# Retention blocks: the state wait behind the intra product, and three rows of the residual stream returned inside the last head

## The chip, the core and the metric

The kernel runs on one core of one Trainium2 chip. The metric is the device time of one execution in microseconds (us), the median over runs. The engines are TensorE (PE: matrix products; PEld: its weight loads), VectorE (DVE), ScalarE (ACT), GpSimd (POOL) and SyncE (SP, which here only issues transfers). Each runs its own instructions in order and they meet through semaphores. SP and ACT each feed one queue of transfers; the same 16 DMA engines serve both. The matrix products run in a format of reduced precision on operands split into a high and a low part, so that one product of full precision is three: high by high, high by low and low by high.

## The reference, cut to what matters

A decoder trunk of four layers works on 1024 prompt positions and 8 sample positions (T = 1032 columns) of width 1024. Layers 0 and 3 are multi-scale retention, layer 1 is differential attention, layer 2 a gated linear recurrence. Each layer is x + W_out(mixer(RMSNorm(x)) * silu(gate)). The change touches layers 0 and 3. There the prompt is cut into eight blocks of 128 positions, and for each of four heads (keys of 256, values of 512) a state S is carried from block to block:

```
s = einsum('bihd,bjhd->bhij', q, k) * decay
o = einsum('bhij,bjhv->bihv', s, v)                 # intra product
o = o + einsum('bihd,bhdv->bihv', q, S0) * q_dec    # state product
S = exp(C*lg) * S0 + einsum('bjhd,bjhv->bhdv', k * k_dec, v)
...
out = (rms_norm(o) * silu(g)) @ w_out
x = x + out
```

The 8 sample positions have one state each, read and written in device memory.

## The kernel before, in words

**Units and chunks.** Activations lie transposed: width on partitions, positions along the free dimension, cut into three chunks of 384, 384 and 264 columns. A unit is 128 output columns of a weight matrix; TensorE makes one unit chunk by chunk, each chunk 8 tiles of three products (`unit_chunk`, lines 301 to 303). Weights go through two raw slots: SP loads one (`load_w`, line 240), ACT copies its high part (`split_hi`, line 248), POOL subtracts for the low part (`split_lo`, line 257), and then the raw slot is free for the next load. Results of a unit go through two PSUM banks in turn.

**A head of retention.** `ret_pe`, `ret_act` and `ret_dve` run the same loop of 36 steps per head (12 units of 3 chunks: 2 of keys, 4 of values, 2 of queries, 4 of the gate). In a step TensorE makes one chunk, and from step 24 on it does in the gate units' shadow, for t = step - 24:
- the four transposes of the output of block t-2 (line 944),
- for block r = t-1: three intra products into the bank OB (953 to 955), for r > 0 the state product on top of it (959, two halves of the key width), then the new contribution to the state into SB0 and SB1 (964 to 966),
- the scores of block t (line 985).

ACT takes block r on: it squares and sums OB (1064), and with DVE's reciprocal root (lines 600 to 607) it scales OB into `onb` (1074), which frees OB. DVE masks the scores (1137), scales the queries (`qdT`, 1144), subtracts for the low part of the scores (`sdl`, 1148), and then folds SB0 and SB1 into the state `St` (1159 and 1160). Semaphores: `r_sd` tells that `sdl` is done, `r_on` that OB is free, `r_qd` that `qdT` is done, `r_su` that `St` holds the block before (and SB0 and SB1 are free), `r_st` that line 966 is done. Before line 953 TensorE waits for `r_sd`, `r_on` and `r_su`; before line 959 for `r_qd`. In step 26 ACT issues four loads of sample states (line 1048) before it goes on with the block. ACT also stores the gate (1028), the normalised output (1058), the sample states (1080) and, after the last block, the prompt's state (1094).

**Where the residual stream goes.** The residual stream `xT` has 8 rows of 128 partitions by 1032 columns. During a retention layer its first six rows (`AWAY_ROWS`) are lent out: `vtl` and `ktl`, the low parts of values and keys, lie there, block after block. The rows come back at the beginning of the output projection (`x_reload`, line 759), from the input in layer 0 and from a copy in device memory (`x_save`) in layer 3. Each row has a semaphore `x_back`, and DVE waits for it before the first addition to that row (`residual_dve`, line 445).

**The output projection.** `out_sp`, `out_act`, `out_dve` and `out_pe` run it in two halves of the input width. Its input, normalised output times gate, is staged from device memory chunk by chunk (`stage_load`, line 414; two slots), DVE multiplies it (`stage_dve`, line 435), ACT copies the high part (334), DVE subtracts for the low part (341). `out_order` begins with units 0 and 1 chunk by chunk, then the other units one after the other. On DVE the order is fixed: fill chunk 0, half of chunk 1, then additions (line 445) with the remaining half fills between them. Each addition frees a PSUM bank.

**What SP issues.** At the end of the last head `out_sp` issues in this order: the first W_out load (it waits for the raw slot); after `r_st` of the last block (`ret_stage_wait`) the stage loads of chunk 0, then row 0; the second W_out load; after the prompt's state has landed (line 707) the stage loads of chunk 1, then row 1; row 2 and the third W_out load; row 3; the stage loads of chunk 2 and the fourth W_out load; row 4, the next half's stage loads, a W_out load; row 5, a W_out load; and so on.

Of the kernel before, what the change touches and what calls it, by code (L numbers as in the profile page):

```python
# [145 lines left out]
def trunk(nc, A, LAYERS=4):  # L146
    ctx = ExitStack()
    with ctx:
# [3 lines left out]
        def sem(name):  # L152
            return ctx.enter_context(nc.semaphore(name))
# [56 lines left out]
        dve_own = sem("dve_own")  # L210
        stage_ld = sems("stage_ld", 4)
        tab_ld, page_cp = sem("tab_ld"), sem("page_cp")
        x_saved, x_back = sem("x_saved"), sems("x_back", KT)

        CR = 2
        CR_PS = 3
# [221 lines left out]
        def residual_dve(dve, unit, q, j, c, final, sqb, sqn, back):  # L438

            c0, w = CHUNKS[c]  # L440
            dve.wait_ge(unit_ps, out_ps(unit, q))
            dve.wait_ge(unit_ev, out_ev(unit, q) - 1)
            if back is not None and c == 0 and j < AWAY_ROWS:
                dve.wait_ge(x_back[j], back)
            nc.vector.tensor_tensor(xT[:, j, c0:c0 + w], bank[q % 2][:, 0:w], xT[:, j, c0:c0 + w], ALU.add)\  # L445
              .then_inc(unit_ev, 1)
            if final:
                dve.wait_ge(sq_done, sqn + 1)
                nc.vector.tensor_tensor(ss[:, c0:c0 + w], ss[:, c0:c0 + w], sqb[:, q % 2, 0:w], ALU.add)\
                  .then_inc(ss_done, 1)  # L450
# [177 lines left out]
        def ret_sp(sp, lay):  # L628
            j_, U, R = lay // 3, UNIT_AT[lay], RAW_AT[lay]
            win, wout = A["ret_w_in"][j_], A["ret_w_out"][j_]  # L630

            def weights(h, js):
                for j in js:
                    col = (h * RDK + (RQK + j * P) if j < 2 else h * RDV + (2 * RQK + (j - 2) * P) if j < 6 else
                           h * RDK + (j - 6) * P if j < 8 else h * RDV + (2 * RQK + RV + (j - 8) * P))
                    load_w(sp, Pos(R, h, RU_IN), j, w_block(win, 0, KT, col))

            def value_rows(h, bs):

                n8, ntr = Pos(8 * RH * j_, h, 8), Pos(RTR * RH * j_, h, RTR)  # L640
                if 0 in bs:
                    sp.wait_ge(r_te, done(ntr.at(17)))
                    sp.wait_ge(r_sn, prior(n8.at(0)))
                    sp.dma_start(v_d, vs[0:NS, :]).then_inc(r_vst, 16)
                    sp.wait_ge(r_vst, Pos(RH * j_, h, 1).at(0) * 16 + 16)
                for b in bs:
                    if b >= 4:
                        sp.wait_ge(r_sn, done(n8.at(b - 4)))
                    sp.dma_start(vbr[:, b % 4, :], v_d[b:b + 1, :].to_broadcast([P, RDV])).then_inc(r_vld[b % 4], 16)

            def page_copies(ns):

                for n in ns:
                    ids = sp.value_load(ptab[0:1, n:n + 1])
                    b, g = divmod(n, PAGES)
                    for cache, dst in ((A["cache_kt"], kc_d), (A["cache_vt"], vc_d)):
                        reg = nc.s_assert_within(ids, 0, cache.shape[1] - 1,
                                                 skip_runtime_bounds_check_because="page ids are rows of the cache")
                        sp.dma_start(dst[b:b + 1, :, :, g, :].rearrange("a h p c -> (a h p) c"),
                                     cache[0, bass.ds(reg, 1), :, :, :].rearrange("a h p c -> (a h p) c"))\  # L660
                          .then_inc(page_cp, 16)

            def head(h):
                sp.wait_ge(r_fo, h + (RH * j_ + 1))
                sp.dma_start(hc, A["c_ret"][bass.ds(h, 1), :, :].rearrange("a p n -> (a p) n")).then_inc(r_hc, 16)
                for j in range(2, 10):
                    weights(h, (j,))
                    if lay == 0:
                        page_copies(range(16 * h + 2 * (j - 2), 16 * h + 2 * (j - 1)))
                    if j == 8:  # L670
                        value_rows(h, range(0, 4))
                weights(h, (10,))
                value_rows(h, range(4, NS))
                weights(h, (11,))

            if lay == 0:
                sp.wait_ge(tab_ld, 16)
            weights(0, (0, 1) if lay else (1,))
            if lay:
                for k in range(KT - 4, AWAY_ROWS):  # L680
                    x_save(sp, UNIT_AT[lay] - KT, k)
                sp.wait_ge(h_raw, fill_tiles(FILL_AT[lay] - 1, 2) + FILL_K[FILL_AT[lay] - 1])
                sp.wait_ge(ss_done, KT * NC_ * (lay + 1))
            sp.dma_start(rsel, A["c_sel"][:, P + 8:P + 16]).then_inc(r_sel, 16)
            for h in range(RH - 1):
                head(h)
                weights(h + 1, (0, 1))
            head(RH - 1)
            out_sp(sp, lay, wout, U + 48, R + 48, [(FILL_AT[lay] + 1, 0), (FILL_AT[lay] + 2, KT)], ret_stage_wait,
                   late_wait=ret_end_wait)  # L690

# [30 lines left out]
        def out_sp(sp, lay, wout, U, R, fills, stage_wait, loaded=0, after=None, late_wait=None):  # L722

            st = stage_of(lay)
            for x, (f, k0) in enumerate(fills):
                kt = FILL_K[f]
                raw = Pos(R + 8 * x)
                if x == 0:
                    for j in range(2):
                        if j >= loaded:  # L730
                            load_w(sp, raw, j, w_block(wout, k0 * P, kt, j * P), kt)
                        if stage_wait is not None:
                            stage_wait(sp, lay, j)
                            stage_load(sp, st, f, k0, j)
                        if lay in (0, 3):
                            x_reload(sp, lay, j)
                    if after is not None:
                        after(sp)
                for j in range(2 if x == 0 else 0, KT):
                    if lay in (0, 3) and x == 0 and j < AWAY_ROWS:  # L740
                        x_reload(sp, lay, j)
                    if lay == 2 and LAYERS > 3 and x + 1 == len(fills) and j >= 4:
                        x_save(sp, U + 8 * x, j - 4)
                    if j == 3:
                        sp.wait_ge(h_raw, fill_tiles(f, 0) + FILL_K[f])
                        stage_load(sp, st, f, k0, 2)
                    if j == 4 and x + 1 < len(fills):
                        sp.wait_ge(h_raw, fill_tiles(f, 1) + FILL_K[f])
                        if late_wait is not None:
                            late_wait(sp, lay)  # L750
                        stage_load(sp, st, *fills[x + 1], 0)
                        sp.wait_ge(h_raw, fill_tiles(f, 2) + FILL_K[f])
                        stage_load(sp, st, *fills[x + 1], 1)
                    load_w(sp, raw, j, w_block(wout, k0 * P, kt, j * P), kt)

        def x_reload(sp, lay, k):

            src = A["x_cols"][k * P:(k + 1) * P, :] if lay == 0 else x_d[k:k + 1, :, :].rearrange("a p t -> (a p) t")
            sp.dma_start(xT[:, k, :], src).then_inc(x_back[k], 16)

        def x_save(sp, U, k):

# [102 lines left out]
        def out_dve(dve, ch, lay, U, fills, last_layer, scale, beside=None, begun=False):  # L865
# [4 lines left out]
            for x, (f, k0) in enumerate(fills):  # L870
# [8 lines left out]
                            clear_sums(dve, ch, lay)  # L879
                    stage_dve(dve, st, f, 1, scale, 0)  # L880
                for q, (j, c) in enumerate(out_order(more or final)):
                    residual_dve(dve, unit, q, j, c, final, sqb, sqn, 16 * (lay // 3 + 1) if lay in (0, 3) and x == 0 else None)
                    sqn += final
                    if q in FILL_BEHIND:
                        stage_dve(dve, st, f, FILL_BEHIND[q][0], scale, FILL_BEHIND[q][1])
# [33 lines left out]
        def ret_pe(pe, lay):  # L919
            f = FILL_AT[lay]  # L920
            def head(h, first):
                unit, raw, n1, n8, ntr = ret_places(lay, h)
                for s in range(36):
# [22 lines left out]
                    if 0 <= t - 1 < NBLK:  # L946
# [2 lines left out]
                            pe.wait_ge(r_te, done(ntr.at(17)))  # L949
                        pe.wait_ge(r_sd, done(n8.at(r)))  # L950
                        pe.wait_ge(r_on, prior(n8.at(r)))
                        pe.wait_ge(r_su, prior(n8.at(r)))
                        nc.tensor.matmul(OB[:, :], sdh[:, r % 2, :], vth[:, r, :], start=True, stop=False)
                        nc.tensor.matmul(OB[:, :], sdh[:, r % 2, :], vtl[:, r, :], start=False, stop=False)
                        last = nc.tensor.matmul(OB[:, :], sdl[:, r % 2, :], vth[:, r, :], start=False, stop=(r == 0))
                        if r:
                            pe.wait_ge(r_qd, done(n8.at(r)))
                            for x in range(2):
                                last = nc.tensor.matmul(OB[:, :], qdT[:, r % 2, x, :], St[:, x, :], start=False,  # L959
                                                        stop=(x == 1))  # L960
# [1278 lines left out]
```

## Time and profile before

| | |
|---|---|
| median of 3 runs | 3273.43 us (3272.81 to 3280.8) |
| profiled execution | 3276.99 us, span 3275.2 us, mean granted clock 0.986 |
| PE, PEld busy | 3120.3 us (95%), 2838.0 us (87%) |
| DVE, ACT, POOL busy | 1372.2 us (42%), 1267.7 us (39%), 561.9 us (17%) |
| transfers | 459.78 MB, mean 140 GB/s |

The span runs from the first to the last instruction of the profiled execution. A busy share is the time in which an engine had an instruction, over the whole span; stages differ. Matmuls are pipelined and their ends are modelled: a matmul's shown time overlaps that of the next. Layer 0 ends near 990 us and layer 3 begins near 2330 us; the last heads' blocks run from about 711 to 778 us and from 2999 to 3066 us.

### The profile page before, as it was taken

What the parts mean: (1) busy time and instruction counts of PE and PEld (TensorE: products, weight loads), DVE (VectorE), ACT (ScalarE), POOL (GpSimd) and SP (SyncE); (2) the same over time, 40 slices, a digit from 0 to 9 for tenths busy, and PEclk for the clock granted to TensorE, in tenths of its full rate; (3) what the DMA queues carried; (4) which work ended last, traced back from release to release, by engine and by line L of the source; (5) the groups of instructions that cost most, each with busy time, mean ns of one, the idle gap of its engine ahead of it and who ended that gap; (6) DMA issues with size and microseconds to landing.
All of it is one profiled execution on the core that took longest, in us unless ns stands there. A gap on an engine that the chain in (4) does not pass through costs nothing.

```text
span 3275.2 us, 51546 instructions
## 1 busy us (share of the span) xinstructions
PE 3120.3 (95%) x19978; PEld 2838.0 (87%) x19978; DVE 1372.2 (42%) x3480; ACT 1267.7 (39%) x2709; POOL 561.9 (17%) x432
## 2 busy tenths in 40 slices
PE   6999999998998999999979899989799999999899
PEld 4989898997997888888859899979798989899799
DVE  3241514226344444444445777763524151422631
ACT  4332423334234555455543455532433332333321
POOL 1112021111211111011101223222111211111121
PEclk8999999999999999999999999999999999999999
DMA  5848586776413444444453122232234242425742
GB/s 164 256 151 248 168 245 194 213 240 224 145 56 116 139 136 155 142 147 143 141 187 100 34 64 63 64 106 82 63 125 129 88 148 89 151 78 163 240 138 80
DMA packets 531892, 459.78 MB, mean 140 GB/s; under 512 B 25091, under 2 KB 464387, under 8 KB 531651
## 3 DMA queue, kind: packets, MB, share of 16 engines
q1 hardware_dynamic: 425570, 334.75, 32.8%
q10 hardware_dynamic: 106080, 121.74, 10.8%
q8 instruction: 160, 2.62, 0.3%
q14 instruction: 82, 0.66, 0.1%
HBM read 354.39 MB, written 169.14 MB: 160 GB/s over the span
## 4 chain that ended last, share of the span: by engine, by line
PE 79%; DVE 10%; issue 4%; ACT 4%; DMA 2%; ACTq 1%; SPq 1%; POOL 0%; DVEq 0%
PE psum L301 20%; PE psum L302 20%; PE psum L303 20%; PE psum L959 3%; PE psum L1419 2%; DVE Hl L341 2%; PE psum L1392 2%; DVE hraw L385 2%; PE psum L936 1%; DVE hraw L435 1%; PE psum L1408 1%; PE psum L1931 1%; PE psum L1462 1%; PE psum L976 1%; PE psum L1431 1%
## 5 line engine op out<-in xcount | busy, mean ns | idle before, releaser
L301 PE MATMUL psum<-Hh,Wh 128*128 128x384 f32 (+1 forms) x4896 | 1633.6, 334 | 92.9 <-DVE Hl L341 31.6
L302 PE MATMUL psum<-Hl,Wh 128*128 128x384 f32 (+1 forms) x4896 | 1574.7, 322 | 0.0
L303 PE MATMUL psum<-Hh,Wl 128*128 128x384 f32 (+1 forms) x4896 | 1574.0, 321 | 0.0
L301 PEld LDWEIGHTS psum<-Hh,Wh 128*128 128x128 f32 x4896 | 931.5, 190 | 147.7 <-issue 55.0
L257 POOL TENSOR_TENSOR Wl<-wraw,Wh 128x512 fp32r<-128x512 f32 (+1 forms) x416 | 533.3, 1303 | 2518.3 <-ACT Wh L248 2517.2
L302 PEld LDWEIGHTS psum<-Hl,Wh 128*128 128x128 f32 x4896 | 932.3, 190 | 6.2 <-issue 0.3
L303 PEld LDWEIGHTS psum<-Hh,Wl 128*128 128x128 f32 x4896 | 930.2, 190 | 0.0
L248 ACT ACTIVATE Wh<-wraw 128x512 fp32r<-128x512 f32 (+1 forms) x416 | 235.1, 615 | 267.3 <-PE psum L303 148.2
L445 DVE TENSOR_TENSOR xT<-psum,xT 128x384 f32<-128x384 f32 x168 | 86.3, 514 | 294.8 <-PE psum L303 294.1
L334 ACT ACTIVATE Hh<-hraw 128x384 fp32r<-128x384 f32 (+1 forms) x252 | 116.5, 489 | 153.8 <-DVE hraw L435 82.4
L1020 ACT ACTIVATE hraw<-psum 128x384 f32<-128x384 f32 (+1 forms) x96 | 44.0, 458 | 279.3 <-PE psum L303 279.3
L1166 DVE SCALAR_TENSOR_TENSOR arena<-arena 128x512 f32<-128x512 f32 x128 | 98.4, 820 | 106.5 <-ACT arena L1069 106.5
L1128 DVE TENSOR_TENSOR vtl<-psum,vth 128x384 fp32r<-128x384 f32 (+1 forms) x96 | 48.6, 506 | 212.0 <-ACT vth L1042 212.0
L1660 ACT ACTIVATE arena<-arena 128x256 f32<-128x256 f32 (+7 forms) x128 | 98.2, 769 | 86.7 <-DVE arena L1725 86.7
L341 DVE TENSOR_TENSOR Hl<-hraw,Hh 128x384 fp32r<-128x384 f32 (+1 forms) x252 | 119.5, 510 | 13.7 <-ACT Hh L334 13.2
L1122 DVE SCALAR_TENSOR_TENSOR ktl<-psum,arena,kth 128x384 fp32r<-128x384 f32 (+1 forms) x48 | 27.5, 573 | 216.8 <-ACT kth L1039 216.8
L1721 DVE CUSTOM_DVE_ANT_0 arena<-psum,arena 128x256 f32<-128x256 f32 (+7 forms) x128 | 91.9, 754 | 47.0 <-PE psum L1392 45.5
L1026 ACT ACTIVATE arena<-psum 128x384 f32<-128x384 f32 (+1 forms) x96 | 44.0, 458 | 166.7 <-PE psum L303 166.7
L959 PE MATMUL psum<-arena 128*128 128x512 f32 x224 | 105.2, 592 | 0.0
L600 DVE TENSOR_SCALAR arena<-arena 128x1 f32<-128x1 f32 x72 | 11.1, 154 | 208.7 <-ACT hraw L1064 208.7
L1074 ACT ACTIVATE arena<-psum,arena 128x512 f32<-128x512 f32 x64 | 44.1, 689 | 117.0 <-DVE arena L607 117.0
L456 ACT ACTIVATE arena<-xT 128x384 f32<-128x384 f32 (+1 forms) x72 | 35.4, 491 | 132.2 <-DVE xT L445 132.2
(212 smaller groups left out, 3164.7 us busy)
## 6 DMA issues: line engine op xcount, KB each, us to landing
wraw<-in_ret_w_in SPq DMA_DIRECT2D x96, 512.0 KB, 4.4
scratch_kc<-in_cache_kt SPq DMA_DIRECT2D x64, 512.0 KB, 6.4
scratch_vc<-in_cache_vt SPq DMA_DIRECT2D x64, 512.0 KB, 6.7
arena<-in_state_ret ACTq DMA_DIRECT2D x64, 512.0 KB, 6.9
out_ret_state_sample<-arena ACTq DMA_DIRECT2D x64, 512.0 KB, 5.1
arena<-scratch_kc SPq DMA_DIRECT2D x64, 512.0 KB, 4.3
arena<-scratch_vc SPq DMA_DIRECT2D x64, 512.0 KB, 4.5
scratch_on<-arena ACTq DMA_DIRECT2D x78, 256.0 KB, 2.4
```

Of the source, the lines that this page charges most:

```text
L248: act.activation(Wh[:, j % 2, x], wraw[:, j % 2, x], ACT.Copy).then_inc(w_hi, 1)
L257: pool.tensor_tensor(Wl[:, j % 2, x], wraw[:, j % 2, x], Wh[:, j % 2, x].bitcast(F32), ALU.subtract)\
L301: nc.tensor.matmul(out, hi, xh, start=(k == 0), stop=False)
L302: nc.tensor.matmul(out, hi, xl, start=False, stop=False)
L303: last = nc.tensor.matmul(out, lo, xh, start=False, stop=(k == kt - 1))
L334: act.activation(Hh[:, k, c0:c0 + w], hraw[:, n % HR, 0:w], ACT.Copy).then_inc(h_hi, 1)
L341: nc.vector.tensor_tensor(Hl[:, k, c0:c0 + w], hraw[:, n % HR, 0:w], Hh[:, k, c0:c0 + w].bitcast(F32), ALU.subtract).then_inc(h_lo, 1)
L445: nc.vector.tensor_tensor(xT[:, j, c0:c0 + w], bank[q % 2][:, 0:w], xT[:, j, c0:c0 + w], ALU.add)\
L959: last = nc.tensor.matmul(OB[:, :], qdT[:, r % 2, x, :], St[:, x, :], start=False, stop=(x == 1))
L1166: last = nc.vector.scalar_tensor_tensor(sring[:, b % 4, x, :], vbr[:, b % 4, :], kT[:, x, SEQ + b:SEQ + b + 1], sring[:, b % 4, x, :], ALU ...
L1660: act.activation(x, x, ACT.Exp, bias=nm2[:, s % 2, m:m + 1], accum_out=(l8[:, s:s + 1], l1[:, s % 2:s % 2 + 1])[m]).then_inc(d_ex, 1)
L1721: nc.vector.tensor_tensor_reduce(out=(S0[t % 3], S1[t % 2])[m][:, 0:W], in0=SSC[m][:, 0:W], in1=strip[:, SEQ - W:SEQ], scale=1.0, scalar=- ...
```

## The change

TensorE's wait for `r_su` moves from line 953 to behind line 955, so that the three intra products come before it. For blocks r > 0 it then stands with the wait for `r_qd` before line 959; for r = 0 it stands before line 964. Rows 0, 1 and 2 are returned by SP at the end of the last head's own issues, behind `r_st` of blocks 2, 4 and 6, when `vtl` and `ktl` of the blocks that lie in a row have been read; the first W_out load comes behind them. Rows 3, 4 and 5 are issued ahead of the third, fourth and fifth W_out load, one place earlier each. Two rows share one `x_back` semaphore, and an addition waits for both.

```diff
-        x_saved, x_back = sem("x_saved"), sems("x_back", KT)
+        x_saved, x_back = sem("x_saved"), sems("x_back", 3)
...
             if back is not None and c == 0 and j < AWAY_ROWS:
-                dve.wait_ge(x_back[j], back)
+                dve.wait_ge(x_back[j // 2], back)
...
             head(RH - 1)
+            for k in range(3):
+                sp.wait_ge(r_st, done(8 * RH * (j_ + 1) - 8 + 2 * k + 2))
+                x_reload(sp, lay, k)
             out_sp(sp, lay, wout, U + 48, R + 48, [(FILL_AT[lay] + 1, 0), (FILL_AT[lay] + 2, KT)], ret_stage_wait,
                    late_wait=ret_end_wait)
...
                             stage_load(sp, st, f, k0, j)
-                        if lay in (0, 3):
-                            x_reload(sp, lay, j)
                     if after is not None:
                         after(sp)
                 for j in range(2 if x == 0 else 0, KT):
-                    if lay in (0, 3) and x == 0 and j < AWAY_ROWS:
-                        x_reload(sp, lay, j)
+                    if lay in (0, 3) and x == 0 and j + 1 < AWAY_ROWS:
+                        x_reload(sp, lay, j + 1)
...
-            sp.dma_start(xT[:, k, :], src).then_inc(x_back[k], 16)
+            sp.dma_start(xT[:, k, :], src).then_inc(x_back[k // 2], 16)
...
-                    residual_dve(dve, unit, q, j, c, final, sqb, sqn, 16 * (lay // 3 + 1) if lay in (0, 3) and x == 0 else None)
+                    residual_dve(dve, unit, q, j, c, final, sqb, sqn, 32 * (lay // 3 + 1) if lay in (0, 3) and x == 0 else None)
...
                         pe.wait_ge(r_sd, done(n8.at(r)))
                         pe.wait_ge(r_on, prior(n8.at(r)))
-                        pe.wait_ge(r_su, prior(n8.at(r)))
                         nc.tensor.matmul(OB[:, :], sdh[:, r % 2, :], vth[:, r, :], start=True, stop=False)
                         nc.tensor.matmul(OB[:, :], sdh[:, r % 2, :], vtl[:, r, :], start=False, stop=False)
                         last = nc.tensor.matmul(OB[:, :], sdl[:, r % 2, :], vth[:, r, :], start=False, stop=(r == 0))
+                        pe.wait_ge(r_su, prior(n8.at(r)))
                         if r:
                             pe.wait_ge(r_qd, done(n8.at(r)))
```

## Rows read from the trace of the kernel before

**Rows 1.** The profile's chain that ended last, shares of the span by engine
```profile
PE 79%; DVE 10%; issue 4%; ACT 4%; DMA 2%; ACTq 1%; SPq 1%; POOL 0%; DVEq 0%
```
**Rows 2.** Waits of TensorE, whole span: total us, times, longest us
```profile
PE psum L953 <- DVE arena L1160: 13.2, 24, 0.7
```
**Rows 3.** TensorE's timeline, block 6 of layer 0's last head: start, us
```profile
763.69 0.60 PE L944 MATMUL psum<-ident,arena 128*128 128x128 f32 x4
...
764.59 0.39 PE L955 MATMUL psum<-vth,sdl 128*128 128x512 f32 x1
764.82 1.88 PE L959 MATMUL psum<-arena 128*128 128x512 f32 x4
...
767.69 0.39 PE L966 MATMUL psum<-vth,ktl 128*128 128x512 f32 x1
```
**Rows 4.** The same, block 7, behind a chunk of 264 columns
```profile
771.28 0.60 PE L944 MATMUL psum<-ident,arena 128*128 128x128 f32 x4
772.44 0.47 PE L953 MATMUL psum<-vth,sdh 128*128 128x512 f32 x1 [0.56 <-DVE arena L1160]
...
773.21 1.88 PE L959 MATMUL psum<-arena 128*128 128x512 f32 x4
```
**Rows 5.** The same, block 2, behind a chunk of 384 columns
```profile
727.94 0.60 PE L944 MATMUL psum<-ident,arena 128*128 128x128 f32 x4
...
729.76 1.88 PE L959 MATMUL psum<-arena 128*128 128x512 f32 x4
```
**Rows 6.** Stretches: five engines' busy us (instructions), granted clock, DMA share, GB/s
```profile
772.00:774.00 2.00, 1.56 (x5) 1.05 (x6) 1.62 (x3) 0.60 (x1) 0.00 (x0) 1.00 0.36 127
3106.00:3110.00 4.00, 3.89 (x20) 3.89 (x21) 3.36 (x10) 1.53 (x4) 0.00 (x0) 0.62 1.04 375
```
**Rows 7.** DVE's timeline, first fill of chunk 2, layer 0
```profile
814.51 1.12 DVE L435 SCALAR_TENSOR_TENSOR hraw<-arena 128x264 f32<-128x264 f32 x3 [3.94 <-DMA arena<-scratch_g]
```
**Rows 8.** TensorE's timeline, unit 0, chunk 2, layers 0 and 3
```profile
818.00 0.39 PE L301 MATMUL psum<-Hh,Wh 128*128 128x264 f32 x1 [2.73 <-DVE xT L445]
...
3106.11 0.39 PE L301 MATMUL psum<-Hh,Wh 128*128 128x264 f32 x1 [2.82 <-DVE xT L445]
```
**Rows 9.** DVE's timeline, blocks 2 and 7 of layer 0's last head
```profile
728.10 0.74 DVE L1160 SCALAR_TENSOR_TENSOR arena<-arena,psum 128x512 f32<-128x512 f32 x1
...
770.69 0.29 DVE L1148 TENSOR_TENSOR sdl<-arena,sdh 128x128 fp32r<-128x128 f32 x1 [0.42 <-ACT sdh L1077]
...
771.55 0.74 DVE L1160 SCALAR_TENSOR_TENSOR arena<-arena,psum 128x512 f32<-128x512 f32 x1
```
**Rows 10.** TensorE's weight loads, block 6 of layer 0's last head
```profile
764.59 0.41 PEld L959 LDWEIGHTS psum<-arena 128*128 128x128 f32 x2
```
**Rows 11.** SP's timeline, last head and output projection, layer 0: start, issue us
```profile
730.39 0.38 SPq L240 DMA_DIRECT2D wraw<-in_ret_w_out  x1
776.52 0.37 SPq L414 DMA_DIRECT2D arena<-scratch_on  x1
...
780.35 1.81 SPq L759 DMA_DIRECT2D xT<-in_x_cols  x1
...
793.82 0.37 SPq L414 DMA_DIRECT2D arena<-scratch_on  x1
...
796.38 1.85 SPq L759 DMA_DIRECT2D xT<-in_x_cols  x2
...
798.76 5.04 SPq L759 DMA_DIRECT2D xT<-in_x_cols  x1
```
**Rows 12.** ACT's timeline, split of the first W_out weight, layer 0
```profile
779.31 1.15 ACT L248 ACTIVATE Wh<-wraw 128x512 fp32r<-128x512 f32 x2
```
**Rows 13.** SP's waits between 700 and 850 us: total us, times, longest
```profile
SPq L707 <- DMA out_ret_state_prompt<-arena: 10.7, 1, 10.7
```
**Rows 14.** Transfers, whole span: issues, KB each, median us to landing
```profile
out_ret_state_prompt<-arena ACTq DMA_DIRECT2D x8, 512.0 KB, 3.2
...
xT<-in_x_cols SPq DMA_DIRECT2D x6, 516.0 KB, 10.8
```

## The prediction, made before the change was run

> **What bounds the kernel now.** I read the chain of waits first: 79% of the span's last-ending chain is TensorE, so time that TensorE stands still is the currency [rows 1]. Next the list of TensorE's waits: block products, line 953, stood still 24 times for the vector engine's state update (line 1160), 13.2 us in all [rows 2]. TensorE's timeline then shows what that costs. A head runs eight retention blocks, one behind each chunk of its last units. In a block that doesn't wait, line 959 starts 1.13 us behind the transposes of line 944 (763.69 to 764.82), with the three intra products (953 to 955) between [rows 3]. Behind a short, 264 column chunk the same way takes 1.93 us (771.28 to 773.21) [rows 4]: 0.80 us is lost where the list shows 0.56, since the transposes' modelled end hides part of it. Going through all 64 blocks of the eight heads, the 24 are always the third, fifth and eighth of a head. The fifth and eighth stand behind short chunks (16 blocks, of which [rows 4] shows one); the third stands behind a long chunk, and ScalarE is late there, since it issues four state loads first (8 blocks; 727.94 to 729.76 is 1.82, so 0.69 lost) [rows 5].
>
> Where the output projection begins I read SyncE's timeline, then the waits of SyncE, DVE and TensorE there. The DMA is busy throughout, at 375 GB/s [rows 6]. The third chunk of the staged inputs comes so late that DVE stands still 3.94 us for it [rows 7], the residual addition is queued behind that fill, and TensorE, which needs the addition's PSUM bank, stands still 2.73 us in layer 0 and 2.82 in layer 3 [rows 8].
>
> **Part 1: the wait for the state, behind the three intra products.** No instruction is added; one wait moves on TensorE's queue, in 64 blocks. The three products read neither state nor state banks; the two of line 959 read the state, and line 964 overwrites the banks. What was late is the update's end at 771.55+0.74 = 772.29 [rows 9], and line 953 started at 772.44, 0.15 later [rows 4]. With the wait moved, the products start behind the transposes and line 959 has two lower limits: its own queue, 771.28+1.13 = 772.41, and the state, seen at 772.44. Its weights are loaded 0.23 ahead of its matmul (764.59 against 764.82) [rows 3, 10]; if that load stands behind the wait and nothing covers it, 772.44+0.23 = 772.67. So it starts between 772.44 and 772.67 instead of 773.21: 0.54 to 0.77 gained. I take 0.66, the middle, times 16 = 10.6. In the third block the limits are 727.94+1.13 = 729.07 and 728.10+0.74+0.15 = 728.99 to 729.22, against 729.76: 0.54 to 0.69, I take 0.62, times 8 = 5.0. Part 1 is 15.6 us.
>
> What is late next? The products also wait for sdl, done at 770.69+0.29 = 770.98, 0.30 before even the transposes start [rows 4, 9]. So the state stays last, by some hundredths, now at line 959. Blocks are not coupled backwards: ScalarE's and DVE's work on a block is released by TensorE's line 959 and 966, so it moves along. Bounds: the two unknowns are how much of the weight load shows and whether the pipe drains. If it drains fully, line 955's last 0.39-0.23 = 0.16 [rows 3] is lost as well: 24 x (0.54-0.16) = 9.1. The far end is 16 x 0.77 + 8 x 0.69 = 17.8. In the other 40 blocks the semaphore is up before and the moved wait costs nothing, as the wait for qdT, already at this place, costs nothing: line 959's weights load right with line 955's matmul, no idle time shown [rows 10].
>
> The Trainium skill (TensorE: Matmul & The Clock Gate, Single matmul latency and Back-to-back issue gap) speaks against: a 512 column product that can't overlap its drain takes (398+512)/2.4 = 379 ns, not 216. As an estimate by that page, if each of the 24 blocks drained, part 1 would be 24 x 0.163 = 3.9 less, 11.7; no row here shows a wait at line 959.
>
> **Part 2: rows 0 to 2 of the residual stream return in the last head.** In layers 0 and 3 SyncE issues them behind blocks 2, 4 and 6 of the last head (about 733, 750 and 768.1: the last is line 966's end, 767.69+0.39, 3.26 behind line 959's start [rows 3]; the first 729.76+3.26 [rows 5]); before, at 780.35 and 796.38 [rows 11]. Three transfers of 516 KB, 1.41 us each at 375 GB/s. Their cover: SyncE issued nothing between 730.39 and 776.52 [rows 11], and the DMA ran at a share of 0.36, 127 GB/s [rows 6]. I cost them at nothing; if contention reached a transfer of that stretch it would be ScalarE's stores, whose buffers it needs again only two blocks, some 17 us, later.
>
> Queued behind the waiting SyncE is one thing: the first W_out load, which moves from 730.39 to 768.1 and behind row 2. ScalarE splits that weight at 779.31 [rows 12]. Two transfers of 0.5 MB are 2.8 us at 375 GB/s; with as much again for other traffic and latency they land near 774, 5 us early: nothing. GpSimd's half of the split follows ScalarE's and moves with nothing. The additions now wait for two rows on one semaphore: rows 0 and 1 are back some 40 us before the first addition, row 3 goes out near 796 and the addition that needs it comes behind 818 [rows 8].
>
> Stream rows 3, 4 and 5 each move up one place, in front of the loads of W_out 2, 3 and 4. So between the second chunk's stage load (793.82) and the third's stand two rows (3, 4) instead of three (1, 2 and 3) [rows 11]: 1.41 us earlier. And row 0 no longer stands among what SyncE issues ahead of the second chunk's load. That load waited 10.7 us for the store of the prompt state to land [rows 13], a store with a median of 3.2 us [rows 14]; it lands when the saturated DMA has drained, so up to 1.41 us earlier again. The third chunk comes 1.4 to 2.8 us earlier, against 2.73 and 2.82 of TensorE's waits: I take 2.4 per layer, nearer the upper end, because the store's landing is what ended that wait [rows 13]. Behind layer 3's wait the granted clock averages 0.62 over 4 us, so most of them at 1.2 GHz instead of 2.4 [rows 6]; that cost up to 0.38 x 4 = 1.5 us, which goes only if the wait does, and I take 0.6. Part 2 is 2 x 2.4 + 0.6 = 5.4, bounds 0 (the third chunk held by something else) and 2.73+2.82+1.5 = 7.1.
>
> The Trainium skill (DMA: Bandwidth & Descriptors, Queues, rings and completion order) says that each DMA engine takes turns between the queues, packet by packet. By that page row 0 in SyncE's queue would hardly delay ScalarE's store, the shift would be 1.4 and part 2, as an estimate, 2 x 1.4 = 2.8. The store's long landing here [rows 13, 14] speaks against even turns.
>
> **Sum.** 15.6+5.4 = 21.0 us. The profiled execution took 3276.99, its span 3275.2 with 1.8 around it, 3.6 above the median of the runs shown. 3276.99-21.0 = 3256.0 in its terms; from the median, 3273.4-21.0 = 3252.4, call it 3252.
>
> **Rivals.**
> A. Only part 1 pays: the DMA stays full, and the third chunk is no earlier. For it: every window there is full. Against: fewer bytes ahead of it. 3273.4-15.6 = 3258. Chance 0.14.
> B. The pipe drains at the new place: part 1 is 9.1, sum 14.5, 3259. For it: 772.44 is a few hundredths behind 772.41, so line 959 does wait. Against: TensorE loads those weights early wherever it isn't blocked [rows 10]. Chance 0.10.
> C. W_out 0 comes late. If it and row 2 each took 10.8 us, the median of the returning rows in the crowded stretch [rows 14], in turn, it would land at 768.1+21.6 = 789.7, 10.4 behind ScalarE's split; ScalarE evicts TensorE's banks in the same queue, so TensorE stands still. Twice 10.4 eats 20.8 of 21.0: 3273, no change. Against: the stretch isn't crowded. Chance 0.04.
> D. Part 1 doesn't do what it says: another wait of line 953 stands as late, and only part 2 is left, 3268. Against: sdl is done before the transposes start [rows 4, 9]. Chance 0.04.
> E. Slower: the wait between lines 955 and 959 breaks the overlap in all 64 blocks, not only where it blocks: 0.16 drain, 0.41/2 = 0.20 weight load [rows 10], 0.15 semaphore, 0.51 x 64 = 33 us, 3273.4-21.0+33 = 3285. It decides from 21.0/64 = 0.33 us per block. Against: the qdT wait at that place. Chance 0.05.
> The forecast has 0.63; its own range is 3247 to 3257.
>
> **How the numbers follow.** Best sum 17.8+7.1 = 24.9, 3248.5; worst of A and B together 9.1, 3264. The range 3245 to 3265 takes these in with 1 to 3 us for the spread of the median, and leaves out C, D and E. A change of 0.3% is 9.8 us, about what can be told from none: forecast, A and B are faster (0.87), C and D the same (0.08), E slower (0.05).
>
> **What would show it.** Line 953's 24 waits are gone, and a wait for line 1160 shows at line 959, if any, of a tenth of a us; short-chunk blocks go from 944 to 959 in 1.15 to 1.4 us. If that stays near 1.9, D; if unblocked blocks grow past 1.13, E. The first W_out load stands near 766, and ScalarE's split isn't preceded by a DMA wait (else C). DVE's wait for the third chunk falls from 3.94 to 1.1 to 2.5 us and TensorE's 2.73 and 2.82 to under 1.4 (else A). The forecast is wrong if part 1 measures under 9 us.

## The result

The changed kernel takes 3254.83 us in the median of 4 runs (3250.32 to 3255.57), beside 3274.26 for the kernel before (4 runs): a ratio of 0.9934, with a 95% interval of 0.9923 to 0.9946, so 19.4 us less. The forecast was 3252, with a range from 3245 to 3265. A second comparison, with 5 runs beside 15 of before, gave 3251.72 against 3275.94, 0.9922 (0.9909 to 0.9936), 24.2 us less.

**The blocks.** The list of TensorE's waits of the changed kernel has no row for line 953 any more, where it had 24 waits [rows 2]. One for the state is left, at the state product (now line 960), twice:

```profile
PE psum L960 <- DVE arena L1161: 0.7, 2, 0.4
```

TensorE's timeline of the changed kernel, block 7 of layer 0's last head, behind a chunk of 264 columns (to be set beside [rows 4]), and below it the last product of the same block in the kernel before:

```profile
760.74 0.60 PE L945 MATMUL psum<-ident,arena 128*128 128x128 f32 x4
...
761.88 1.93 PE L960 MATMUL psum<-arena 128*128 128x512 f32 x4
...
764.81 0.40 PE L967 MATMUL psum<-vth,ktl 128*128 128x512 f32 x1
```
```profile
776.09 0.39 PE L966 MATMUL psum<-vth,ktl 128*128 128x512 f32 x1
```

From transposes to state product it takes 1.14 us, where it took 1.93, and where a block that waits for nothing takes 1.13 [rows 3]. Two more rows of the same block of the changed kernel show why: DVE's state update, and TensorE's weight load.

```profile
761.03 0.74 DVE L1161 SCALAR_TENSOR_TENSOR arena<-arena,psum 128x512 f32<-128x512 f32 x1
```
```profile
761.82 0.30 PEld L960 LDWEIGHTS psum<-arena 128*128 128x128 f32 x2 [0.23 <-DVE arena L1161]
```

The state is done at 761.77, and the weights of the state product load 0.05 later, at 761.82. Unblocked they would load at 761.65, 0.23 ahead of the matmul. So the load is late, as the row's wait says, and the first matmul behind it isn't: it starts at 761.88, 0.01 behind its own queue's limit of 760.74+1.13 = 761.87. Over the 56 blocks with a state product, the way from the transposes to that product sums to 82.2 us before and 65.0 now, 17.2 less.

Not all of that is kept, since the late load shows one matmul later. The four matmuls of the state product take 1.93 us here and 1.88 where nothing waits [rows 3]. The last product of the block starts 764.81-760.74 = 4.07 behind the transposes: before it was 776.09-771.28 = 4.81, and in a block that doesn't wait it is 767.69-763.69 = 4.00 [rows 3]. Up to their last products the 56 blocks gain 16.2 us.

**The output projection.** SyncE's timeline of the changed kernel, layer 0 (start, us of issue; to be set beside [rows 11]):

```profile
723.32 0.33 SPq L760 DMA_DIRECT2D xT<-in_x_cols  x1
...
757.59 0.33 SPq L760 DMA_DIRECT2D xT<-in_x_cols  x1
757.96 0.43 SPq L240 DMA_DIRECT2D wraw<-in_ret_w_out  x1
765.23 0.38 SPq L414 DMA_DIRECT2D arena<-scratch_on  x1
...
781.48 0.36 SPq L414 DMA_DIRECT2D arena<-scratch_on  x1
```

Chunk 1's stage loads go out 16.25 us behind chunk 0's, where it was 17.30 (793.82-776.52). DVE's and TensorE's timelines at the third chunk, layer 0 and then layer 3 (to be set beside [rows 7, 8]):

```profile
801.20 1.12 DVE L435 SCALAR_TENSOR_TENSOR hraw<-arena 128x264 f32<-128x264 f32 x3 [1.91 <-DMA arena<-scratch_g]
```
```profile
804.68 0.39 PE L301 MATMUL psum<-Hh,Wh 128*128 128x264 f32 x1 [0.70 <-DVE xT L445]
...
3085.79 0.39 PE L301 MATMUL psum<-Hh,Wh 128*128 128x264 f32 x1 [0.36 <-DVE xT L445]
```

From the last state product to this point it takes 42.80 us in layer 0 (before: 818.00-773.21 = 44.79) and 42.48 in layer 3 (before 45.16). The granted clock behind it in layer 3 (engines' busy us, then clock, DMA share, GB/s; to be set beside [rows 6]) stays at 2.4 GHz, 1.00 instead of a mean of 0.62:

```profile
3085.80:3089.80 4.00, 3.88 (x29) 3.67 (x30) 3.66 (x10) 1.90 (x5) 0.00 (x0) 1.00 1.06 375
```

ScalarE's split of the first W_out weight follows its neighbour without a wait, so the load that moved from 730.39 to 757.96 is in time:

```profile
767.94 0.20 ACT L1088 ACTIVATION_READ_ACCUMULATOR arena<-psum 128x1 f32 x1
768.03 1.15 ACT L248 ACTIVATE Wh<-wraw 128x512 fp32r<-128x512 f32 x2
```

**The account of the two traces.** The span is 3253.8 against 3275.2, 21.4 less: 16.0 in the retention heads (layer 0 from 607.74 to 598.85, layer 3 from 607.67 to 600.55, each from the first transposes of an output to the last state product), 2.0 and 2.7 where the projections begin, 1.1 from layer 3's third chunk to the end, 2.4 ahead of these; against that it took 2.8 more between layer 0's third chunk and layer 3's heads.

### The profile page after: what moved, and what is told of

Its sections match the earlier page's. It is cut to its first block, busy times and chain, and to the rows that moved or that the text cites. A ratio compares the mean times of both kernels' runs of the same rounds, so it can differ in the third digit from the quotient of the medians.

```text
span 3253.8 us, 51594 instructions
## 1 busy us (share of the span) xinstructions
PE 3120.5 (96%) x19978; PEld 2838.7 (87%) x19978; DVE 1369.5 (42%) x3480; ACT 1267.6 (39%) x2709; POOL 560.8 (17%) x432
## 4 chain that ended last, share of the span: by engine, by line
PE 84%; DVE 8%; ACT 3%; issue 3%; DMA 2%; SPq 1%; POOL 0%; ACTq 0%; DVEq 0%
PE psum L301 21%; PE psum L302 21%; PE psum L303 21%; PE psum L960 3%; PE psum L1393 2%; PE psum L1420 2%; DVE Hl L341 2%; DVE hraw L385 2%; PE psum L937 1%; PE psum L1409 1%; DVE hraw L435 1%; PE psum L1932 1%; PE psum L1463 1%; PE psum L1432 1%; PE psum L977 1%
```

## The experiments

**1. The changed kernel again**, to see whether the 2.8 us in layers 1 and 2 belong to the change.

> The changed kernel once more, beside its parts on one chip. The first comparison gave 19.4 us between the medians; the two traces give 17.45 in the 56 blocks with a state product and 2.0+2.7 where the output projections begin, 22 in all, while the rest of the span (the start, layers 1 and 2) differs by parts of 2 to 3 us either way. Theory: those are chance, so this run's trace shows other differences there and 20 to 22 us between the medians. Rival: layers 1 and 2 give back 2.8 us because of the change; then this trace shows 2.8 us more in them again.

Measured: 24.2 us less than before (above). From layer 0's last state product to layer 3's first transposes it took 1677.5 us; it was 1680.07 before and 1680.88 in the first trace of the changed kernel. This trace lost nothing there: 2.6 less than before, of which the third chunk of layer 0 is 1.7. So the 2.8 are chance and no price of the change. From layer 0's third chunk to layer 3's first transposes the ten traces of this document take 1629.9 to 1638.1 us. The expectation's 17.45 is 17.2: one third block of layer 3 was taken for 1.57 us and lasts 1.84.

**2. The wait alone**: the kernel before with this edit.

```diff
-                        pe.wait_ge(r_su, prior(n8.at(r)))
                         nc.tensor.matmul(OB[:, :], sdh[:, r % 2, :], vth[:, r, :], start=True, stop=False)
...
+                        pe.wait_ge(r_su, prior(n8.at(r)))
```

> Only the wait moved, the rows return as before. Theory: the two parts add up; 24 blocks go from about 1.9 to 1.14 us, 17 to 18 us less in all, and TensorE's waits of 2.73 and 2.82 us at the third chunk stay. Rival 1 (the prediction's sizes): 15.6. Rival 2 (what the blocks gain waits elsewhere, in the ring of weights or at the end of the head): under 10 between the medians although the blocks are shorter.

Measured: 3260.77 against 3275.94, 0.9952 (0.9938 to 0.9965), 15.2 less; the ways from the transposes to the state product sum to 65.0 us, 17.2 less, and the heads of both layers take 16.2 less. The third chunk's waits stay, 3.05 and 2.37 us, and so does the clock's drop behind the second (here it falls behind the first too, to a mean of 0.60 from 807 to 811 us):

```profile
3084.90:3088.90 4.00, 4.00 (x22) 4.00 (x23) 3.21 (x9) 1.53 (x4) 0.00 (x0) 0.62 1.05 376
```

The gain doesn't come back as a wait of like size. The interval, 11.5 to 20.3 us, is too wide to tell 15.6 from the expected 17 to 18; in the trace the state products start 17.2 earlier in sum, and 16.2 of it stays in the heads.

**3. The rows alone**: the changed kernel with the wait back ahead of the three products.

```diff
+                        pe.wait_ge(r_su, prior(n8.at(r)))
                         nc.tensor.matmul(OB[:, :], sdh[:, r % 2, :], vth[:, r, :], start=True, stop=False)
...
-                        pe.wait_ge(r_su, prior(n8.at(r)))
```

> Only the rows moved, the wait stands before the block's products as before. Theory: 4 to 5 us less; DVE's wait for the third chunk 3.94 to about 1.9 us, TensorE's 2.73 and 2.82 to under 1; line 953 waits 24 times again, 13 us shown. Rival (the transfer is hidden anyway and the gain at the third chunk came with the shorter blocks): no change, under 1 us.

Measured: 3268.93 against 3275.94, 0.9978 (0.9969 to 0.9987), 7.0 less, with an interval from 4.3 to 10.2. The list of TensorE's waits has the 24 again (the products are one line lower):

```profile
PE psum L954 <- DVE arena L1161: 13.0, 24, 0.7
```

At the third chunk TensorE waits 1.20 and 0.16 us, and layer 3's clock stays up behind it:

```profile
3099.10:3103.10 4.00, 3.86 (x29) 3.64 (x30) 3.67 (x10) 1.87 (x5) 0.00 (x0) 1.00 1.05 375
```

The 1.20 is above the expected "under 1". So the rows pay by themselves, a little more than expected, and the parts add: 15.2+7.0 = 22.2 beside 24.2 for both.

**4. One product ahead of the wait** instead of three.

```diff
                         nc.tensor.matmul(OB[:, :], sdh[:, r % 2, :], vth[:, r, :], start=True, stop=False)
+                        pe.wait_ge(r_su, prior(n8.at(r)))
                         nc.tensor.matmul(OB[:, :], sdh[:, r % 2, :], vtl[:, r, :], start=False, stop=False)
                         last = nc.tensor.matmul(OB[:, :], sdl[:, r % 2, :], vth[:, r, :], start=False, stop=(r == 0))
-                        pe.wait_ge(r_su, prior(n8.at(r)))
```

> The changed kernel with the wait for the state behind the first of the three intra products instead of the third. Theory (a product ahead of the wait covers as much as the step between two products' starts, 0.31 for the first, and weight loads cost nothing): the 24 blocks take 1.93-0.31 = 1.6 us from line 944 to the state product instead of 1.14, so 24 x 0.46 = 11 us more than the changed kernel, 9 to 10 less than before. Rival (the pipe drains at a wait inside the product): 0.16 to 0.2 us per block worse than that, 4 to 5 us in all, so 5 less than before.

Measured: 3263.31 against 3275.94, 0.9954 (0.994 to 0.9968), 12.6 less; 11.6 above the changed kernel of the same comparison. TensorE's timeline of this kernel, block 7 of layer 0's last head:

```profile
767.74 0.60 PE L945 MATMUL psum<-ident,arena 128*128 128x128 f32 x4
...
768.82 0.50 PE L955 MATMUL psum<-vtl,sdh 128*128 128x512 f32 x1 [0.24 <-DVE arena L1161]
...
769.38 1.88 PE L960 MATMUL psum<-arena 128*128 128x512 f32 x4
```

From transposes to state product it takes 1.64 us, where the product's cover gives 1.62 and a drained pipe 1.8. A wait between products costs what it waits here, and nothing on top; rival B of the prediction falls with it. The four matmuls of the state product, whose weights don't come late here, take 1.88 us again instead of 1.93. The distance to the changed kernel is the 11 that was expected; 12.6 below the kernel before is more than the expected 9 to 10.

**5. No row ahead of the third chunk**: row 3 goes out behind its stage loads, rows 4 and 5 at their old places.

```diff
-                    if lay in (0, 3) and x == 0 and j + 1 < AWAY_ROWS:
-                        x_reload(sp, lay, j + 1)
+                    if lay in (0, 3) and x == 0 and 3 < j < AWAY_ROWS:
+                        x_reload(sp, lay, j)
...
                         stage_load(sp, st, f, k0, 2)
+                        if lay in (0, 3) and x == 0:
+                            x_reload(sp, lay, 3)
```

> The changed kernel with row 3 returned behind the third chunk's stage loads and rows 4 and 5 at their places of before, so that no row stands between the second chunk's stage loads and the third's. Theory (rows ahead of the third chunk delay it, 1.41 us each): DVE's wait for the third chunk, 1.1 to 2.3 us in the changed kernel, goes to 0, and TensorE's wait before it, 0 to 1.0, too; 1 to 2 us less than the changed kernel over both layers. Rival (chunk 3 is held by its own 2 MB in a full DMA): the wait stays above 1.

Measured: 3249.38 against 3274.38, 0.9921 (0.9907 to 0.9935). DVE has no wait for a transfer left there; its fill follows the addition at once:

```profile
800.35 0.55 DVE L445 TENSOR_TENSOR xT<-psum,xT 128x384 f32<-128x384 f32 x1
800.82 1.11 DVE L435 SCALAR_TENSOR_TENSOR hraw<-arena 128x264 f32<-128x264 f32 x3
```

TensorE's wait at the third chunk is gone in both layers. The mechanism holds in the trace. The time, 25.0 less than before, can't be told from the changed kernel's 24.2.

**6. Row 0 back at its old place**, a single run.

```diff
-            for k in range(3):
+            for k in range(1, 3):
...
                             stage_load(sp, st, f, k0, j)
+                        if lay in (0, 3) and j == 0:
+                            x_reload(sp, lay, 0)
```

> The changed kernel with row 0 alone returned at its old place, behind the first chunk's stage loads. It tells what row 0 did to the second chunk's stage loads, which wait for the store of the prompt's state. Theory (the store lands when the full DMA has drained): those loads go out 17.3 us behind the first chunk's again, against 16.3 and 15.7 in the changed kernel. Rival (each DMA engine takes turns between the queues, so SyncE's row hardly delays ScalarE's store): they stay at 15.7 to 16.3.

SyncE's timeline of this kernel, layer 0:

```profile
768.23 0.38 SPq L414 DMA_DIRECT2D arena<-scratch_on  x1
...
771.64 1.28 SPq L762 DMA_DIRECT2D xT<-in_x_cols  x1
...
785.56 0.37 SPq L414 DMA_DIRECT2D arena<-scratch_on  x1
```

17.33 us, and 17.42 in layer 3: the distances of before (17.30 and 17.42). Row 0, in SyncE's queue, does delay the landing of ScalarE's store, and with it these loads, by 1.1 and 1.7 us against the changed kernel (16.25 and 15.68); the store lands 8.9 and 9.0 us behind its issue here and before, 7.8 and 7.2 in the changed kernel. TensorE's waits at the third chunk are 1.96 and 1.54 here, between the two kernels'. The time, 3260.56, is of one run and decides nothing.

**7. ScalarE's four state loads in two steps.** In layer 3's heads 2 and 3 (counted from 0) the third block took 1.84 us each in the changed kernel, since ScalarE spent 2.94 and 3.04 us on issuing four loads there, 1.99 elsewhere.

```diff
-                    for b in (range(4) if s == 12 else range(4, NS) if s == SREAD_AT[0] + 1 else []):
+                    for b in (range(4) if s == 12 else range(4, 6) if s == 26 else range(6, NS) if s == 27 else []):
```

> The changed kernel with ScalarE's four loads of sample states spread over two steps, two in step 26 and two in step 27. Theory: the third block of layer 3's heads 2 and 3 took 1.56 to 1.84 us in three traces with the moved wait, since ScalarE spent 2.6 to 3.2 us on issuing the four loads there; with two loads ahead of the block both take 1.14 and layer 3's heads 599 us instead of 600 to 600.5; 1 to 1.5 us less than the changed kernel. Rival (the long issue is an instruction fetch that falls there by chance of position): it moves to another block, no gain.

Measured: 3250.13 against 3274.38, 0.993 (0.9917 to 0.9944). Layer 3's heads take 598.66 us, as layer 0's do, and no third block is late (1.13, 1.14). ScalarE's timeline of this kernel, step 26 of head 3 of layer 3, where head 2 has 0.94 us:

```profile
2986.14 2.17 ACTq L1049 DMA_DIRECT2D arena<-in_state_ret  x2
```

A long issue remains in head 3, so its cause isn't the four in a row; it is only covered now. The rival holds in part: in layer 0 two issues of step 27 took 1.93 and 1.86 us, and one fourth block 1.26. The trace confirms a gain of 1.6 to 1.9 us in layer 3's heads beside the two traces of the changed kernel, the medians can't. What makes the issue long there stays open.

**8. Both of the last edits.**

> The last two edits of this list together on top of the changed kernel: no row ahead of the third chunk, and the four loads in two steps. Theory: the gains add, 2 to 3.5 us less than the changed kernel, so some 25 to 27 us less than before. Rival: each is below what can be told, and the sum is within 1 us of the changed kernel.

Measured: 3249.0 against 3274.38, 0.9921 (0.9908 to 0.9935), 25.4 less. It is the lowest median, but within 1.2 us of 5 and 7, and not to be told from the changed kernel (24.2 less in its own comparison): nearer the expectation's second case.

## Why the prediction was right, step by step

**Part 1** was put at 15.6 us. By the starts of the state products it measures 17.2, by the last products of the blocks 16.2, and the heads take 16.0 less. The mis-sized term is the weight load: I let half of its 0.23 us show, and it costs 0.06 per block. The weights do load late and the first matmul starts almost as if they hadn't, but the matmuls behind it come later (1.93 us for the four instead of 1.88), and the block stays that much late. The rest of the step is as told: the state is last, by hundredths; sdl and the freed bank are not late. The Trainium skill's longer time for a product that can't overlap its drain (TensorE: Matmul & The Clock Gate, Single matmul latency) doesn't show: a block loses 0.06 us, not the 0.16 worked out from it. Nothing is given back elsewhere, as the prediction had it: in layer 0 the blocks gain 8.9 up to their last products, and the heads 8.9. In layer 3 the heads gain 7.1. There, about 1.6 is missing in two third blocks, 1.84 us each where the prediction had 1.13 to 1.28: ScalarE's long issue makes the state late again, and experiment 7 took that away. That the total came so near 15.6 is partly luck: the load put too high and the two late blocks offset each other.

**Part 2** was put at 5.4: 2.4 per layer and 0.6 for the clock. The traces give 2.0, 2.7 and 1.1, 5.8 in sum. Both mechanisms are shown apart, in the traces: the row among the first loads (experiment 6) and the rows ahead of the third chunk (5). The clock term was undersized, since the wait fell to 0.36 and with it the whole drop; with waits of 2.37 [experiment 2] and 2.82 [rows 8] the mean was 0.62, with 0.36 and 0.16 it was 1.00. From layer 3's third chunk to the end it takes 169.1 and 169.0 us in the two traces with that drop and 168.0 in the changed kernel. The length of the wait alone doesn't decide it: behind layer 0's 2.73 us [rows 8] the clock stayed at 1.00, and behind 1.96 us in experiment 6 it fell to a mean of 0.66 over 4 us; what decides stays open. By the turns between queues of the Trainium skill (DMA: Bandwidth & Descriptors, Queues, rings and completion order), as I read them, row 0 would have had hardly any effect. Experiment 6 shows 1.1 and 1.7 us, and can't tell why.

**Rivals.** A falls by experiment 3, B by 4, C by ScalarE's split without a wait, D by the 17.2, E by the blocks that wait for nothing: 1.13 us as before. The early rows cost nothing that a trace shows: layer 3's heads take 607.61 us with the rows alone and 607.67 without.

**The sum** of 21.0 lies between the two measured differences, 19.4 and 24.2; its terms measure 16.0+5.8 = 21.8 in the traces. The stretch with layers 1 and 2 alone varies by some 8 us from trace to trace, so the agreement of the sum is worth less than that of its terms.

## What to carry to other kernels

A wait belongs in front of the first instruction that needs it, not in front of its group: move it behind as much independent work as the wait is long, and count the gain from start to start, up to the last product of the group: a pipelined engine's list of waits (13.2 us here) understates it (16.2), and the start of the first product behind the wait overstates it (17.2). When a queue is full, a transfer that nobody needs yet is paid for by whatever is issued behind it, and also by a store in another queue for which that queue waits; look for a stretch in which the queue stands idle, and send it there.

## What the hardware showed that I had not expected

A weight load that began 0.17 us late (761.82 instead of 761.65) moved the start of the matmul behind it by 0.01 us, but made the four matmuls of the state product take 1.93 us instead of 1.88. The same four load issues took ScalarE 1.99 us in six heads, and 2.59 to 3.29 in layer 3's heads 2 and 3 in the five traces that have the whole wait moved and the four in a row; the same two heads took 1.99 and 2.2 before.
